# Rows of an expert block fill eight of sixteen partition groups first, then the other eight

## The reference

```python
grp = argmax(h @ wg + bg)                     # one of 4 groups
top_v, top_i = top_k(le of that group, 2)     # 2 of its 8 experts
wts = softmax(top_v) * p_grp
# every token is a row of two experts: 2048 rows, 32 experts
y[row] = (silu(x @ w1[e]) * (x @ w3[e])) @ w2[e]
out[token] += wts * y[row]
x = x + g2 * out;  return rmsnorm(x, norm_f)
```

## Time and profile before

| what | us |
|---|---|
| median of three runs | 1740.2 (1734.2 to 1742.88) |
| the profiled execution | 1736.56 |
| its span, first to last instruction | 1734.8 |
| TensorE busy | 1609.8 (93%) |
| VectorE busy | 674.0 (39%) |
| ScalarE busy | 404.2 (23%) |
| GpSimd busy | 176.7 (10%) |
| weight queue q1 / row queue q0, share of 16 DMA engines over the span | 49.4% / 6.1% |

### The profile page before, as it was taken

How to read it: one execution, slowest core, us unless ns; L and a number is a source line. 1 busy time by engine, 2 the same in 40 slices (tenths; PEclk the granted TensorE clock), 3 DMA queues, 4 the chain that set the end, 5 groups by cost and what they waited for, 6 DMA issues and landing times. The chain is left out here.

```text
span 1734.8 us, 37173 instructions
## 1 busy us (share of the span) xinstructions
PE 1609.8 (93%) x15961; PEld 1042.2 (60%) x15961; DVE 674.0 (39%) x1682; ACT 404.2 (23%) x897; POOL 176.7 (10%) x220
## 2 busy tenths in 40 slices
PE   5999999998999999999999999989999999998873
PEld 3444445886777776644444445557777767666652
DVE  3533324213667666776555365571000100000003
ACT  4100000002666666510100003221212111111112
POOL 1205000000111010000000000001111111111100
PEclk9999999998999999999999999999999999999997
DMA  9874233145201008424543172179999999999996
GB/s 343 261 228 107 74 97 124 50 139 147 62 3 45 32 2 251 138 73 130 148 122 90 30 291 85 61 273 392 384 385 393 398 389 383 401 394 404 405 389 235
DMA packets 163745, 362.38 MB, mean 209 GB/s; under 512 B 28631, under 2 KB 111183, under 8 KB 138971
## 3 DMA queue, kind: packets, MB, share of 16 engines
q1 hardware_dynamic: 141456, 316.12, 49.4%
q0 software_dynamic: 12608, 28.01, 6.1%
q10 hardware_dynamic: 9516, 15.85, 2.6%
HBM read 323.48 MB, written 48.50 MB: 214 GB/s over the span
## 5 line engine op out<-in xcount | busy, mean ns | idle before, releaser
L2817 PE MATMUL psum<-sb_m_xT,sb_m_ring 128*64 128x64 f32 (+2 forms) x4096 | 151.8, 234 | 20.1 <-issue 15.8
L2817 PEld LDWEIGHTS psum<-sb_m_xT,sb_m_ring 128*64 128x64 f32 x4096 | 148.0, 139 | 33.3 <-issue 32.0
L2701 DVE TENSOR_TENSOR sb_m_hT<-psum,sb_m_sg 128x256 f32<-128x256 f32 (+2 forms) x32 | 15.3, 477 | 306.9 <-PE psum L2817 306.9
L2538 ACT ACTIVATE sb_m_xT<-psum,sb_rowmod 128x64 f32<-128x64 f32 (+2 forms) x256 | 81.9, 426 | 208.2 <-PE psum L2805 208.2
L849 PE MATMUL psum<-sb_vD,sb_room 128*128 128x512 f32 x240 | 104.7, 592 | 0.2 <-DVE sb_vD L730 0.2
L2817 PE MATMUL psum<-sb_m_xT,sb_front 128*64 128x64 f32 (+2 forms) x2560 | 94.7, 233 | 8.8 <-issue 6.0
L2817 PEld LDWEIGHTS psum<-sb_m_xT,sb_front 128*64 128x64 f32 x2560 | 91.3, 139 | 17.3 <-issue 16.6
L1147 ACT ACTIVATE sb_d_probs<-sb_d_probs,sb_d_nmax 128x640 f32<-128x640 f32 (+7 forms) x128 | 92.8, 735 | 13.4 <-DVE sb_d_nmax L1188 12.8
L2824 PE MATMUL psum<-sb_m_ring,sb_m_hT 128*64 128x512 f32 (+2 forms) x256 | 84.1, 611 | 2.7 <-DVE sb_m_hT L2701 1.4
L1714 PE MATMUL psum<-sb_w_o_sb,sb_room 128*128 128x512 f32 x192 | 84.0, 593 | 0.0
L849 PEld LDWEIGHTS psum<-sb_vD,sb_room 128*128 128x128 f32 x240 | 45.5, 190 | 57.9 <-issue 57.9
(11 more groups left out here) (441 smaller groups left out, 2501.9 us busy)
## 6 DMA issues: line engine op xcount, KB each, us to landing
sb_m_ring<-in_exp_w_dram SPq DMA_DIRECT2D x48, 2048.0 KB, 31.8
sb_front<-in_exp_w_dram SPq DMA_DIRECT2D x30, 2048.0 KB, 29.8
sb_rows<-in_exp_w_dram SPq DMA_DIRECT2D x18, 2048.0 KB
sb_g_ada<-in_ada_w_dram SPq DMA_DIRECT2D x16, 1024.0 KB, 5.2
d_qk<-sb_n_b_sel ACTq DMA_DIRECT2D x20, 512.0 KB, 3.3
sb_front<-in_w_in_dram SPq DMA_DIRECT2D x16, 512.0 KB, 5.5
sb_front<-d_qk SPq DMA_DIRECT2D x15, 512.0 KB, 6.9
sb_n_b_sel<-in_w_in_dram SPq DMA_DIRECT2D x10, 512.0 KB, 8.9
```

The lines of the kernel that those rows point to most:

```text
L2538: last = act.activation(dst[:, kk, 0:w], src, ACT.Identity, scale=k.rowmod[:, 0, kk:kk + 1], bias=k.rowmod[:, 1, kk:kk + 1])
L2817: mm = pe.matmul(k.psum[part, which, c * w:(c + 1) * w], view[:, kk, first:first + 2 * CAPS - 1:2], x[:, kk, 0:w], start=(kk == 0), stop=( ...
```

## The change

Twice eight groups in place of sixteen. CELL is 8, so `lane` is n mod 8 and `turn_no` n div 8. As long as turn_no is under step, rows are dealt to eight groups; from then on (`upper`) to the other eight, with turn_no counted from 0 again. The lane of a row is moved by 8 where exactly one of two things holds: the lane is 5 or 7, or the row is among the upper ones. So the first eight groups are 0, 1, 2, 3, 4, 6, 13 and 15, the others 8, 9, 10, 11, 12, 14, 5 and 7. In odd pairs the order of the lanes within the eight is reversed as before. Groups, widths and steps are the same as before. A full block is full in either kernel; in one that is not, the places without a row are now all in the second eight groups, as long as those have enough. `first_order` is made in two halves, with four small corrections for the groups 5, 7, 13 and 15.

```diff
--- before.py
+++ after.py
@@ -1781,7 +1781,7 @@
 SPARE = RING - 2
 ROUND = 12582912.0
 PAD = 4 * S
-CELL = 16
+CELL = 8
 
 
 def block_order():
@@ -2183,10 +2183,15 @@
             v.inc(tt(chosen.wts[:, 0], er, pg, ALU.mult)); v.wait(dve)
             v.inc(tt(chosen.wts[:, 1], chosen.wts[:, 0], ev, ALU.mult))
             v.inc(ts(chosen.row0, both[:, 0:NT, 0], -float(PAD), float(PAD), ALU.mult, ALU.add))
-            per = CAPM // CELL
-            v.inc(stt(first_order[:, :].rearrange("p (e q) -> p e q", e=CELL),
-                      const(K_M128, per).unsqueeze(1).to_broadcast([P, CELL, per]), CELL / P,
-                      const(K_I128, CELL).unsqueeze(2).to_broadcast([P, CELL, per]), ALU.mult, ALU.add))
+            per = CAPM // (2 * CELL)
+            for g in range(2):
+                v.inc(stt(first_order[:, CAPM // 2 * g:CAPM // 2 * (g + 1)].rearrange("p (e q) -> p e q", e=CELL),
+                          const(K_M128, per).unsqueeze(1).to_broadcast([P, CELL, per]), CELL / P,
+                          const(K_I128 + CAPM // 2 * g, CELL).unsqueeze(2).to_broadcast([P, CELL, per]), ALU.mult, ALU.add))
+            v.wait(dve)
+            for lane, other in ((5, CAPM / 2), (7, CAPM / 2), (13, -CAPM / 2), (15, -CAPM / 2)):
+                at = first_order[:, per * lane:per * (lane + 1)]
+                v.inc(ts(at, at, float(other), None, ALU.add))
 
             dve.wait_ge(s_rank, 2)
             e = slice(0, NE)
@@ -2634,7 +2639,7 @@
             v.inc(tt(wider, past, wider, ALU.subtract)); v.wait(dve)
             v.inc(ts(cell, cell, ROUND, None, ALU.subtract))
             v.inc(ts(pair_of, pair_of, ROUND, None, ALU.subtract))
-            v.inc(stt(step, wider, float((CAPW - CAPM) // CELL), narrow, ALU.mult, ALU.subtract)); v.wait(dve)
+            v.inc(stt(step, wider, float((CAPW - CAPM) // (2 * CELL)), narrow, ALU.mult, ALU.subtract)); v.wait(dve)
             v.inc(stt(lane, cell, -float(CELL), dest, ALU.mult, ALU.add))
             v.inc(stt(turn_no, pair_of, -float(P // CELL), cell, ALU.mult, ALU.add))
             v.inc(ts(odd, pair_of, 0.5, -0.25, ALU.mult, ALU.add)); v.wait(dve)
@@ -2647,9 +2652,18 @@
             v.inc(stt(odd, odd, -2.0, pair_of, ALU.mult, ALU.add))
             v.inc(tt(turn_no, turn_no, upper, ALU.subtract)); v.wait(dve)
             v.inc(tt(back, back, odd, ALU.mult))
+            v.inc(ts(step, step, float(CAPM // (2 * CELL)), None, ALU.add))
             v.inc(stt(dest, turn_no, 1.0 - CELL, dest, ALU.mult, ALU.add)); v.wait(dve)
-            v.inc(tt(lane, lane, back, ALU.add)); v.wait(dve)
-            v.inc(stt(lane, step, float(CAPM // CELL), lane, ALU.add, ALU.mult)); v.wait(dve)
+            v.inc(tt(lane, lane, back, ALU.add))
+            v.inc(tt(upper, turn_no, step, ALU.is_ge)); v.wait(dve)
+            v.inc(ts(odd, lane, -6.0, None, ALU.add))
+            v.inc(tt(back, upper, step, ALU.mult)); v.wait(dve)
+            v.inc(tt(odd, odd, odd, ALU.mult))
+            v.inc(tt(dest, dest, back, ALU.subtract)); v.wait(dve)
+            v.inc(stt(odd, odd, 1.0, upper, ALU.is_equal, ALU.subtract)); v.wait(dve)
+            v.inc(tt(odd, odd, odd, ALU.mult)); v.wait(dve)
+            v.inc(stt(lane, odd, float(CELL), lane, ALU.mult, ALU.add)); v.wait(dve)
+            v.inc(tt(lane, step, lane, ALU.mult)); v.wait(dve)
             v.inc(tt(dest, dest, lane, ALU.add)); v.wait(dve)
             v.inc(ts(quot, dest, 1.0 / CAPS, 0.5 / CAPS - 0.5, ALU.mult, ALU.add)); v.wait(dve)
             v.inc(ts(unit, quot, ROUND, None, ALU.add)); v.wait(dve)
```

## The result

The kernel after takes 1743.3 us, the median of 20 runs (1737.2 to 1746.0), where the kernel before on the same chip takes 1740.0. The ratio is 1.0022 with a 95% interval of 1.0012 to 1.0032: slower by some 3 to 4 us, inside the 0.5% that the prediction calls the same, but on the other side of zero than its 4.2 us of gain.

The account below looks back on a forecast made before the run. The DMA engines finishing last were taken as the bound: 4.5 us sooner, less 0.3 for TensorE's chain, nothing added for VectorE, sums to -4.2 us, from 1740.2 to 1736.0 us, range 1728 to 1745.

Parts of the forecast that it names:

- The bound: Expert stage, 1150 to 1698 us: the DMA engines finishing last set the end; half of them lag about 12 us.
- What moves and its price: Row gathers and additions: 8.5 rows per engine move, at 0.53 us a row, 4.5 us each way.
- Small blocks neutral: In small blocks groups L and L+8 share two engines, so nothing shifts; otherwise the shift would be 22.75 rows per engine.
- The chosen groups are the early engines: The eight groups filled first sit on the early DMA engines, so the late ones end 4.5 us sooner; chance 0.50.
- Its argument from 13 and 15: Choosing 13 and 15 in place of 5 and 7 leaves small blocks even only if L and L+8 share engines.
- Rival (b): Chosen groups are not the early engines; even one misplaced makes late engines end 4.5 us later, 1744.7 us; chance 0.15.
- the even cut: In big blocks, a gather's 80 or 112 partitions are split evenly over 16 engines, so group L is engine L's share.
- The gain with the right eight: Last weight landing 4.5 us sooner, less 0.3 us for TensorE's own chain and stalls: 4.2 us gained.
- 10.7 us of waits for weights: TensorE's weight waits from 1600 to 1700 us, from which it could give back the time as loads end sooner.
- VectorE: Row-place table grows from three dependent steps to eight at 0.21 us, 1.4 us in all, hidden by the load queue.
- What would show it: In the profile after: half-share tail cut from 12 to about 3 us, TensorE's late weight waits some 4 us less or shifted.

Follow-up runs that it names:

- e2: The kernel after with groups 2 and 3 also changing sides with 10 and 11; ratio to before 1.0036.
- e3: The kernel after with groups 3 and 4 also changing sides with 11 and 12; ratio to before 1.0025.
- e4: The kernel after with groups 2 and 4 also changing sides with 10 and 12; ratio to before 1.0027.
- f1: The kernel after with nothing exchanged, so groups 0 to 7 are filled first; ratio to before 1.0019.
- f2: The kernel after with only 6 and 7 exchanged, so 0 to 5, 14 and 15 are filled first; ratio to before 1.0019.
- f3: The kernel after with only 5 and 6 exchanged, so 0 to 4, 7, 13 and 14 are filled first; ratio to before 1.0024.
- f4: The kernel after with only 0 and 7 exchanged, so 1 to 6, 8 and 15 are filled first; ratio to before 1.0034.
- g1: Against the kernel after, big blocks fill groups 0 to 5, 8 and 13 first, small blocks 0 to 7; ratio to before 1.0028.
- g2: Against the kernel after, big blocks fill groups 0 to 4, 6, 8 and 14 first, small blocks 0 to 7; ratio to before 1.0018.
- h3: h1's lanes, but big blocks fill groups 5, 6 and 9 to 14 first; 1744.7 us against before's 1739.3, ratio 1.0030.
- e1: Rows placed as in the kernel before, with the change's longer VectorE arithmetic to no effect; 1736.9 us against before's 1738.6, ratio 0.9989.
- h2: h1's places in big blocks, but small blocks fill groups 8 to 15 first; 1735.5 us, ratio to before 0.9982.
- g3: Against the kernel after, big blocks fill groups 0 to 4, 7, 8 and 15 first, small blocks 0 to 7; 1737.9 us, before 1739.2, ratio 0.9992.
- h1: g3's places made with seven dependent steps fewer on VectorE; 1737.5 us against before's 1739.3, ratio 0.9993.

## Why the prediction went wrong, point by point

**The bound: right for the loss.** The DMA engines that finish last set the end. All eleven kernels with a late engine loaded (after, e2 to e4, f1 to f4, g1, g2, h3) have their last landing at 551.7 to 553.8 us and ratios of 1.0018 to 1.0036. The three with the right eight have it at 545.9 to 547.2, with 0.9982 to 0.9993. In finer steps the medians don't follow it: before and e1 land at 548.1 and 549.5, and e1's ratio is 0.9989.

**What moves and its price: right.** After separates four kinds of engine, and their distances need no common zero. Early engines land at 529.9 relieved and at 539.2 loaded (means of two and of the first six of the twelve, by the groups worked out above), late ones at 542.6 relieved and 551.9 loaded. Loaded less relieved is 9.3 us in both, 4.65 for each way, where 8.5 rows x 0.53 gave 4.5. The other six kernels with two late engines loaded give 9.0 to 10.1 in the same way. The queue's share over the stage hardly moved, against the earlier trace rows:

```profile
q1 hardware_dynamic: 25751, 197.17, 88.0%
q0 software_dynamic: 6848, 16.58, 12.2%
```

**Small blocks neutral: right.** h2 shows it, with no view of before to read it from. The Trainium skill, "DMA: Bandwidth & Descriptors", section "The descriptor swizzle", gives partitions 0 to 3 and 32 to 35 of a 128-partition transfer to one engine, and 64 to 67 and 96 to 99 to another. Cut like that, groups L and L + 8 of a small block have the same two engines; h2 agrees with it.

**The chosen groups are the early engines: this step failed.** The prediction gave it half of the chances with no row behind it; it said itself that the rows tell that half of the engines lag and not which. Its argument from 13 and 15 is about how small blocks are cut, and says nothing of which engines are early. The step was right for six of the eight groups; 6 and 13 are on late engines. Rival (b) names what happened: late engines get 8.5 rows more, and one misplaced is as bad as eight, +4.5 us and 1744.7. Measured are 1743.3 us, with two misplaced: 3.3 over before and not 4.5. e1 shows that the loss is that of the places, and g3 against g1 and g2 that it is that of the groups. The mechanism on the late side was right; the chances, 0.50 against 0.15, were set the wrong way. With a choice of eight out of sixteen and a rule by which a single miss decides, the slower side should have had the larger one.

Rival (b) leaned beside that on the Trainium skill, "DMA: Bandwidth & Descriptors", section "Latency and other measured facts", by which engines 7 and 15 are usually the slower ones. The runs disagree: the late ones here are eight, and those that serve groups 7 and 15 of the big blocks are early. That these are the engines 7 and 15 is the even cut that the prediction assumed; no view names them.

**The gain with the right eight: smaller than forecast, and its size is open.** The forecast wanted 4.2 us from such a set. By their medians g3, h1 and h2 are 1.3, 1.8 and 3.8 us under before, 2.3 in the mean, but e1, which moves no row, is 1.7 under by the same measure. So the medians don't show that g3 or h1 gained anything. The last landings do show an earlier end of the loads: 547.2, 545.9 and 546.4 us, where before and e1 have 548.1 and 549.5, 0.9 to 3.6 us sooner and not 4.5. Two things make it less. With all eight shifted, the gap between the means of the first and the last eight landings fell from 11.9 and 12.4 (before, e1) to 4.9, 4.9 and 4.6, and in h3 rose to 19.8: about 7.5 us, 3.8 each way, and not 4.65. The three kernels with four late engines loaded give 6.7 to 8.7 for both ways together, 8.2 in the mean, between the 9.3 of two and this 7.5. And the late class is not one number: its last member decides, and its eight landings are spread over 2.7 and 2.9 us in before and e1, over 3.9 to 4.4 in the three. (Where the two classes meet, these figures take the last eight landings for the late ones.) Why whole classes shift by less than single engines is open.

The prediction also let TensorE get the time back from its 10.7 us of waits for weights. It did not: from 1180 to 1710 they are 10.2 to 10.8 us in g3, h1 and h2, as in before. From the last landing to the end of the span it is 32.8 to 36.2 us over all the profiled executions, a scatter of the size of the gain.

**VectorE: right in its steps, and hidden as forecast.** The eight dependent steps are there; the last are 0.21 us from start to start (VectorE in time):

```profile
1162.99 0.18 DVE L2657 TENSOR_TENSOR sb_rows<-sb_rows 128x16 f32<-128x16 f32 x1
...
1164.29 0.18 DVE L2665 SCALAR_TENSOR_TENSOR sb_rows<-sb_rows 128x16 f32<-128x16 f32 x1
1164.50 0.17 DVE L2666 TENSOR_TENSOR sb_rows<-sb_rows 128x16 f32<-128x16 f32 x1
1164.71 0.17 DVE L2667 TENSOR_TENSOR sb_rows<-sb_rows 128x16 f32<-128x16 f32 x1
```

The loads that wait for the tables come 19.0 us after the stage's first and before 18.5, 0.5 us later, where 1.4 was worked out. Single executions scatter here: e1, f1, f3 and f4, with as many steps, have 19.0 too, and f2 20.3. e1 has no loss, and g3 none with loads at 22.7.

**What would show it: half useful.** The shape of the tail told the cause at once. TensorE's waits for weights did not, in the stretch that the prediction named. In after they are these, from 1600 to 1710 (us in total, times, longest), 8.4 us against 10.7 in the earlier trace rows, in a kernel that is slower:

```profile
PE psum L2831 <- DMA sb_m_ring<-in_exp_w_dram: 3.8, 3, 1.5
PE psum L2831 <- DMA sb_front<-in_exp_w_dram: 2.7, 1, 2.7
...
PE psum L2831 <- DMA sb_rows<-in_exp_w_dram: 1.0, 1, 1.0
PE psum L2838 <- DMA sb_m_ring<-in_exp_w_dram: 0.9, 1, 0.9
```

The rest lies ahead of that stretch. From 1180 to 1600 after has these, 4.3 us, and before has none:

```profile
PE psum L2831 <- DMA sb_rows<-in_exp_w_dram: 1.8, 1, 1.8
...
PE psum L2831 <- DMA sb_m_ring<-in_exp_w_dram: 1.4, 2, 1.0
...
PE psum L2831 <- DMA sb_front<-in_exp_w_dram: 0.7, 1, 0.7
PE psum L2838 <- DMA sb_m_ring<-in_exp_w_dram: 0.4, 1, 0.4
```

Together that is 12.7 us against 10.7. Before 1600 the waits tell the kernels apart: none in before, g3, h1 and h2, 0.8 us in e1, 1.2 to 5.2 in the eleven that are slower. TensorE's busy time in a fixed window does not. It was busy for 115.30 us from 1180 to 1300, where it was 116.69; but moved by the 3.35 us by which the stage starts later, to 1183.35 to 1303.35, the window holds 116.39.

## What to carry to other kernels

Where all 16 DMA engines are full and a load lands in 16 pieces, as here, the last piece sets the time. So a shift of work between engines gains only if every engine that gets more is an early one. Two misplaced of eight, the fewest tried, turned a small gain into a loss of 0.2%, and four or eight cost no more that the intervals could tell. Before work is moved between engines, the trace has to say which piece of data goes by which of them: the landings of one load, sorted, in kernels that differ in two groups each, gave that here. A set that looks deliberate is no evidence that it is the right one. And a kernel that moves nothing (e1) tells how small a gain can still be believed: it came out 0.1% faster.

## What the runs showed of the hardware that was not expected

- Under a full weight queue with gathers and additions beside it, half of the DMA engines finish 11.9 to 12.4 us after the other half over some 547 us (before, e1). It is not the rows: by the counts of the prediction every group has 67 to 69 rows of the big blocks, and the late eight together 543 against 550 of the early ones. The late ones belong to groups 5, 6 and 9 to 14, and all kernels on all four chips fit that; in four pairs L and L + 8 differ, in two both are late and in two both early. What makes them late was not found. One candidate was not tried: from 1150 to 1700 the instruction queue q8 takes 0.8% of 16 engines, some 70 engine-us, against 95 by which the late eight lag (8 x 11.9), and no view says on which engines its packets go.
- With the right eight filled first, the spread of one load's 16 landings grows more slowly through the stage: 4 us after 297 us (294.0 to 297.8 in g3) where it was 8 (290.7 to 298.8 before), and 9 at the end where it was 14.
- The moment at which the expert stage begins differs by up to 6 us between single executions of these kernels (1150.4 to 1156.7), more than the change is worth. Counted from the stage's first load to the end of the span, one execution of each gives 579.5 to 580.3 us in g3, h1 and h2, 583.5 and 584.4 in e1 and before, 585.2 to 590.0 in all others. The ratios of the medians tell only the last kind from the other two.
